# Attention scores with 128 contraction rows, in two products instead of three, and the second head pair's projections in other PSUM banks

## The reference, cut to what matters

```python
z = jnp.einsum('bqhd,bkhd->bhqk', q_blk.astype(jnp.float32), kf) * scale
# stick-breaking heads
strict = key_pos[None, :] < q_pos[:, None]
log_beta = jax.nn.log_sigmoid(z)
...
# forgetting heads (q and k are RMS-normalised per head first)
z = z + jnp.moveaxis(f_q, 1, 2)[..., None] - f_keys[:, :, None, :]
p = jax.nn.softmax(jnp.where(causal, z, -jnp.inf), axis=-1)
```

## Time and profile before

| | |
|---|---|
| median of 3 runs | 1152.43 us (1151.81 to 1153.05) |
| profiled execution, its own time | 1151.13 us |
| its span | 1149.4 us |
| mean granted clock of TensorE | 0.998 |
| PE busy | 1129.6 us (98%) |
| DVE busy | 582.7 us (51%) |
| ACT busy | 435.9 us (38%) |
| POOL busy | 62.3 us (5%) |
| the mixer, about | 422 to 727 us of the span |

### The profile page before, as it was taken

The page is one execution under the profiler, slowest core; times in us unless marked ns, Lnnn a source line. Parts: engine busy times, 40 slices in busy tenths (PEclk is TensorE's granted clock), DMA queues, the critical chain, the costliest instruction groups (busy, mean ns, idle before and its releaser), DMA issues.

```text
span 1149.4 us, 14368 instructions
## 1 busy us (share of the span) xinstructions
PE 1129.6 (98%) x5206; PEld 896.3 (78%) x5206; DVE 582.7 (51%) x813; ACT 435.9 (38%) x677; POOL 62.3 (5%) x48
## 2 busy tenths in 40 slices
PE   8999999999999998999999999999999999999997
PEld 5788888888788867788778777778888888878876
DVE  3745555555644465666665566673333333433343
ACT  5422222222222234566775665352232322221322
POOL 1000000000000001000000000000000000225350
PEclk9999999999999999999999999999999999999999
DMA  9655765675573731222212111332333333223231
GB/s 344 209 147 164 204 198 164 166 202 164 165 212 106 192 91 40 71 56 56 55 38 68 44 37 37 92 92 74 91 91 91 91 91 94 89 65 110 83 110 74
DMA packets 168918, 131.21 MB, mean 114 GB/s; under 512 B 5180, under 2 KB 150700, under 8 KB 168876
## 3 DMA queue, kind: packets, MB, share of 16 engines
q1 hardware_dynamic: 168704, 130.60, 38.8%
q10 hardware_dynamic: 172, 0.06, 0.0%
HBM read 128.54 MB, written 2.10 MB: 114 GB/s over the span
## 4 chain that ended last, share of the span: by engine, by line
PE 93%; DVE 3%; ACT 2%; DMA 1%; issue 1%; DVEq 0%; POOL 0%; SPq 0%; ACTq 0%; POOLq 0%
PE bank L662 29%; PE bank L664 28%; PE bank L663 28%; PE bank L950 1%; PE bank L975 1%; PE bank L682 1%; DVE w_lo L1424 1%; DMA w_raw<-in_w_ffn_down_dram 1%; PE bank L928 1%; ACT w_hi L1070 1%; PE bank L715 1%; PE bank L1008 0%; PE bank L708 0%; DVE y L1879 0%; PE bank L740 0%
## 5 line engine op out<-in xcount | busy, mean ns | idle before, releaser
L1424 DVE TENSOR_TENSOR w_lo<-w_raw,w_hi 128x1024 fp32r<-128x1024 f32 x163 | 215.1, 1321 | 387.9 <-ACT w_hi L1070 387.7
L662 PE MATMUL bank<-h_hi,w_hi 128*128 128x512 f32 x864 | 350.0, 405 | 3.9 <-DVE v_lo L1725 3.6
L664 PE MATMUL bank<-h_hi,w_lo 128*128 128x512 f32 x864 | 342.9, 397 | 0.0
L663 PE MATMUL bank<-h_lo,w_hi 128*128 128x512 f32 x864 | 342.9, 397 | 0.0
L1070 ACT ACTIVATE w_hi<-w_raw 128x1024 fp32r<-128x1024 f32 x163 | 172.2, 1058 | 424.7 <-PE bank L664 396.0
L662 PEld LDWEIGHTS bank<-h_hi,w_hi 128*128 128x128 f32 x864 | 163.3, 189 | 46.9 <-issue 8.1
L663 PEld LDWEIGHTS bank<-h_lo,w_hi 128*128 128x128 f32 x864 | 163.3, 189 | 40.7 <-issue 2.9
L664 PEld LDWEIGHTS bank<-h_hi,w_lo 128*128 128x128 f32 x864 | 163.1, 189 | 39.5
L563 POOL TENSOR_TENSOR w_raw<-w_raw,gate_row 128x1024 f32<-128x1024 f32 (+1 forms) x24 | 56.0, 2334 | 627.2 <-DMA w_raw<-in_w_ffn_down_dram 626.8
L662 PE MATMUL bank<-w_hi,hid_hi 128*128 128x512 f32 x176 | 69.8, 397 | 2.2 <-DVE w_lo L1424 2.2
L662 PE MATMUL bank<-hid_hi,w_hi 128*128 128x512 f32 x176 | 70.2, 399 | 1.3 <-DVE w_lo L1424 1.3
(11 more groups left out here) (201 smaller groups left out, 1339.9 us busy)
## 6 DMA issues: line engine op xcount, KB each, us to landing
w_raw<-in_w_ffn_up_dram SPq DMA_DIRECT2D x88, 512.0 KB, 4.8
ada_w<-in_w_ada_dram SPq DMA_DIRECT2D x56, 512.0 KB, 3.8
w_raw<-in_w_ffn_down_dram SPq DMA_DIRECT2D x36, 512.0 KB, 4.5
w_raw<-in_w_in_dram SPq DMA_DIRECT2D x28, 512.0 KB, 3.9
ada_first<-in_w_ada_dram SPq DMA_DIRECT2D x16, 512.0 KB, 10.2
w_raw<-in_w_out_dram SPq DMA_DIRECT2D x8, 512.0 KB, 3.7
w_raw<-in_w_ffn_down_dram SPq DMA_DIRECT2D x8, 384.0 KB, 4.7
x_nat<-in_x_dram SPq DMA_DIRECT2D x4, 512.0 KB, 4.8
```

Of the source, the lines that this page charges most:

```text
L662: mm(dst, wh, xh, start=start, stop=False, skip_group_check=skip)
L663: mm(dst, wh, xl, start=False, stop=False, skip_group_check=skip)
L664: return mm(dst, wl, xh, start=False, stop=stop, skip_group_check=skip)
L1424: v.tensor_tensor(w_lo[:, s, :], w_raw[:, r, :], w_hi[:, s, :].bitcast(F32), ALU.subtract)\
```

## The change

The stationary operand of a segment gets 128 rows: the head's high part of q in its own 64 partitions and the low part in the other 64 (`q_st`). The moving operand of the first product is the high part of k in both halves (`k_hh`): its second half is made by a transfer inside SBUF that GpSimd issues (`repeat_k`), once ACT has written the high part (`k_made`). The moving operand of the second product is the low part of k with zero rows in the other half (`k_l`). These two replace the three. ACT and DVE write the parts in two instructions of 64 partitions each instead of one of 128. GpSimd clears the zero rows when FFN 1's last tile has been used, and issues the first job's copies between its memsets. `f_cum` and `rowsel` get 128 rows, of which the new ones are zero. q1 and k1 are put in banks 6 and 7, and the values and statistics of job 0 wait until those have been read. `k_hh` and `k_l` of even jobs lie in the room of the last heads' outputs, and the split of v0's first weight tile lies in that of the first.

```diff
-        out.append((kind, n, {"v": 0, "q": 0, "k": 1, "g": n % 2}[kind] + (6 if kind in "qk" and n == 0 else 0), tile))
+        out.append((kind, n, {"v": 0, "q": 0, "k": 1, "g": n % 2}[kind] + (6 if kind in "qk" and n <= 1 else 0), tile))
...
-        rowsel_f = keep("rowsel_f", [HD, JOBS])
-        rowsel = keep("rowsel", [HD, JOBS], F32R)
+        rowsel_f = keep("rowsel_f", [P, JOBS])
+        rowsel = keep("rowsel", [P, JOBS], F32R)
...
-        qk_hi = keep("qk_hi", [P, 2, 2, SEQ], F32R)
-        qk_lo = keep("qk_lo", [P, 2, 2, SEQ], F32R)
+        q_st = keep("q_st", [P, 2, 2, SEQ], F32R)
+        k_hh_b = keep("k_hh_b", [P, 2, SEQ], F32R)
+        k_l_b = keep("k_l_b", [P, 2, SEQ], F32R)
         pt_hi = keep("pt_hi", [P, 2, PT_BLOCKS, P], F32R)
         pt_lo = keep("pt_lo", [P, 2, PT_BLOCKS, P], F32R)
+        o_offset = top[0]
         o_hi = keep("o_hi", [P, JOBS, SEQ], F32R)
         o_lo = keep("o_lo", [P, JOBS, SEQ], F32R)
+        k_hh_a = at("k_hh_a", [P, 2, SEQ], F32R, o_offset + (JOBS - 2) * SEQ * 4)
+        k_l_a = at("k_l_a", [P, 2, SEQ], F32R, o_offset + (2 * JOBS - 2) * SEQ * 4)
+        k_hh, k_l = (k_hh_a, k_hh_b), (k_l_a, k_l_b)
         beyond = top[0]
         f_keys = keep("f_keys", [P, 2, SEQ])
-        f_cum = keep("f_cum", [HD, SEQ], F32R)
+        f_cum = keep("f_cum", [P, SEQ], F32R)
...
-        w4_hi = at("w4_hi", [P, WS], F32R, region + 2 * FC * SEQ * 4)
-        w4_lo = at("w4_lo", [P, WS], F32R, region + 2 * FC * SEQ * 4 + WS * 4)
+        w4_hi = at("w4_hi", [P, WS], F32R, o_offset)
+        w4_lo = at("w4_lo", [P, WS], F32R, o_offset + WS * 4)
...
-        mix_zero = sem("mix_zero")
+        mix_zero, k_zero = sem("mix_zero"), sem("k_zero")
+        k_twice = [sem("k_twice0"), sem("k_twice1")]
...
+        def k_made(j):
+
+            if j >= SBJ:
+                return nrm_hi, norm_of("k", j) + 1
+            ci = [c for c, chunk in enumerate(CHUNKS) if chunk[0:2] == ("k", j)][0]
+            until = STEPS.index(("evac", ci))
+            return chunk_hi, 1 + sum({"v": 2, "q": 1, "k": 1, "g": 0}[CHUNKS[step[1]][0]]
+                                     for step in STEPS[:until] if step[0] == "evac")
+
...
+            def repeat_k(j):
+
+                pool.wait_ge(*k_made(j))
+                g.dma_start(k_hh[j % 2][HD:P, 0, :].bitcast(F32), k_hh[j % 2][0:HD, 0, :].bitcast(F32))\
+                    .then_inc(k_twice[j % 2], 16)
+                g.dma_start(k_hh[j % 2][0:HD, 1, :].bitcast(F32), k_hh[j % 2][HD:P, 1, :].bitcast(F32))\
+                    .then_inc(k_twice[j % 2], 16)
+
+            pool.wait_ge(w_used, T_MIX)
+            for n, part in enumerate((k_l_a[HD:P, 0, :], k_l_a[0:HD, 1, :], k_l_b[HD:P, 0, :], k_l_b[0:HD, 1, :])):
+                g.memset(part.bitcast(F32), 0.0).then_inc(k_zero, 1)
+                pool.wait_ge(k_zero, n + 1)
+
             pool.wait_ge(h_done, 2 * KC)
...
                 pool.wait_ge(mix_zero, n + 1)
+                if n == 0:
+                    repeat_k(0)
+            for j in range(1, JOBS):
+                repeat_k(j)
...
+                        if j == 0:
+                            pe.wait_ge(k_zero, 4)
+                        pe.wait_ge(k_twice[j % 2], 32 * (j // 2 + 1))
...
-                        rows = slice(h * HD, (h + 1) * HD)
-                        q_h, q_l = (q[rows, j % 2, 0, i * P:(i + 1) * P] for q in (qk_hi, qk_lo))
-                        k_h, k_l = (k[rows, j % 2, 1, 0:n] for k in (qk_hi, qk_lo))
-                        three(zb[:, c0:c0 + n], q_h, q_l, k_h, k_l, True, False)
+                        qs = q_st[:, j % 2, h, i * P:(i + 1) * P]
+                        mm(zb[:, c0:c0 + n], qs, k_hh[j % 2][:, h, 0:n], start=True, stop=False)
+                        mm(zb[:, c0:c0 + n], qs, k_l[j % 2][:, h, 0:n], start=False, stop=False)
...
+                        pe.wait_ge(*chunk_read(last_on_bank[6]))
...
+                    else:
+                        pe.wait_ge(*chunk_read(last_on_bank[7]))
...
-                    mm(bank[7][:], rowsel[:, head:head + 1].broadcast_to([HD, P]), f_cum[:], start=True, stop=True)\
+                    mm(bank[7][:], rowsel[:, head:head + 1].broadcast_to([P, P]), f_cum[:], start=True, stop=True)\
...
-                        a(qk_hi[:, n % 2, int(what == "k"), :], bank[b][:], ACT.Copy,
-                          scale=0.125 if what == "q" else 1.0).then_inc(chunk_hi, 1)
+                        for h in range(2):
+                            rows = slice(h * HD, (h + 1) * HD)
+                            if what == "q":
+                                last = a(q_st[rows, n % 2, h, :], bank[b][rows, :], ACT.Copy, scale=0.125)
+                            else:
+                                last = a(k_hh[n % 2][rows, h, :], bank[b][rows, :], ACT.Copy)
+                        last.then_inc(chunk_hi, 1)
...
-                        a(qk_hi[:, n % 2, int(what == "k"), :], nrm[:], ACT.Copy,
-                          scale=gq8[:] if what == "q" else col(R_GK)).then_inc(nrm_hi, 1)
+                        for h in range(2):
+                            rows = slice(h * HD, (h + 1) * HD)
+                            if what == "q":
+                                last = a(q_st[rows, n % 2, h, :], nrm[rows, :], ACT.Copy, scale=gq8[rows, :])
+                            else:
+                                last = a(k_hh[n % 2][rows, h, :], nrm[rows, :], ACT.Copy, scale=col(R_GK)[rows, :])
+                        last.then_inc(nrm_hi, 1)
...
-                        v.scalar_tensor_tensor(qk_lo[:, n % 2, int(what == "k"), :], bank[b][:],
-                                               0.125 if what == "q" else 1.0,
-                                               qk_hi[:, n % 2, int(what == "k"), :].bitcast(F32),
-                                               ALU.mult, ALU.subtract).then_inc(qk_ready, 1)
+                        for h in range(2):
+                            rows, other = slice(h * HD, (h + 1) * HD), slice((1 - h) * HD, (2 - h) * HD)
+                            if what == "q":
+                                last = v.scalar_tensor_tensor(q_st[other, n % 2, h, :], bank[b][rows, :], 0.125,
+                                                              q_st[rows, n % 2, h, :].bitcast(F32),
+                                                              ALU.mult, ALU.subtract)
+                            else:
+                                last = v.tensor_tensor(k_l[n % 2][rows, h, :], bank[b][rows, :],
+                                                       k_hh[n % 2][rows, h, :].bitcast(F32), ALU.subtract)
+                        last.then_inc(qk_ready, 1)
...
-                        v.scalar_tensor_tensor(qk_lo[:, n % 2, int(what == "k"), :], nrm[:],
-                                               gq8[:] if what == "q" else col(R_GK),
-                                               qk_hi[:, n % 2, int(what == "k"), :].bitcast(F32),
-                                               ALU.mult, ALU.subtract).then_inc(nrm_lo, 1)
+                        for h in range(2):
+                            rows, other = slice(h * HD, (h + 1) * HD), slice((1 - h) * HD, (2 - h) * HD)
+                            if what == "q":
+                                last = v.scalar_tensor_tensor(q_st[other, n % 2, h, :], nrm[rows, :], gq8[rows, :],
+                                                              q_st[rows, n % 2, h, :].bitcast(F32),
+                                                              ALU.mult, ALU.subtract)
+                            else:
+                                last = v.scalar_tensor_tensor(k_l[n % 2][rows, h, :], nrm[rows, :], col(R_GK)[rows, :],
+                                                              k_hh[n % 2][rows, h, :].bitcast(F32),
+                                                              ALU.mult, ALU.subtract)
+                        last.then_inc(nrm_lo, 1)
```

## The result

The changed kernel takes 1145.63 us (median of 5 runs, 1145.08 to 1148.20). The kernel before took 1152.43 us on the same chip (5 runs, 1151.56 to 1154.29). The ratio is 0.9943, 95% interval 0.9928 to 0.9958: faster by 6.8 us, where 26.2 were forecast, and outside the range of 1121 to 1138. The profiled execution took 1145.88 us, its span is 1144.1.

A forecast was written before the change was run, and what follows sets the result against it. The prediction took the mixer for a PE-bound stream. Gross savings of 10.2 + 7.8 + 6.0 + 1.6 + 5.3 = 30.9 us less 4.7 of losses gave 26.2, so 1126.2 us, range 1121 to 1138.

The forecast's parts named there:

- The products removed: Scores on PE: one product fewer in each of 64 segments, 10.2 us saved.
- the ways in: Scores on PE: entering 64-row products after transposes or a mask costs extra; 7.8 us saved, bounds 0 and 7.8.
- the ways out: Scores on PE, second product to mask: leaving 64-row products costs extra; 6.0 us saved, bounds 0 and 6.0.
- rival A: Scores on PE: float transposes and bfloat mask, not height, cause the extra time; gain 11, 1141 us; chance 0.12.
- the late weight load: Mask product on PE: its weight load starting late looked like a drain, so the full 6.0 us was taken.
- The banks' term: Job 0, q1 and k1 in banks 6 and 7: the v0 wait and low clock behind it go, 5.3 us.
- rival C: First scores of five jobs: copies come late; gain 7 at 8.1 us, 1159 us at 11 us; chance 0.05.
- decay products: Eight PE products going from 64 to 128 rows, an entry and an exit each: 1.6 us saved, bounds 0 and 1.6.
- theory L: Formed after the measurement: in jobs 0 to 3 a closed DVE and ACT loop, longer than PE's shortened unit, lost the gain.
- just met: Statistics products after a head's values: six of sixteen have little slack before a PE that comes earlier, 1.5 us lost.
- Rival B: Mixer: evacuations' second halves aren't hidden, PE waits 10 us more at transposes and statistics; gain 16, 1136 us; chance 0.13.
- Job 0's start: Job 0's first transposes and weight tiles: split evacuations make ACT and DVE later, 2.2 us lost, bounds 0 and 5.

The follow-up runs named there:

- banks-only kernel: The kernel before with only q1 and k1 in banks 6 and 7 and the two waits that guard them: 1147.61 us, ratio 0.9955.
- both remedies: Changed kernel with q and k evacuations in one 128-partition instruction per engine and the absolute value ahead of relu; scores partly of wrong rows: 1123.55 us, ratio 0.9759.
- one-piece kernel: Changed kernel with q's and k's parts written in one instruction of 128 partitions on ACT and on DVE; scores of other numbers: 1130.20 us.
- absolute value first: Changed kernel with ACT's absolute value as soon as a unit's scores are made and DVE's relu after it: 1132.87 us, ratio 0.9827.
- one piece on DVE: Changed kernel with DVE's low parts of q and k in one 128-partition instruction, ACT's high parts still in two: 1134.37 us, ratio 0.9848.
- one piece on ACT: Changed kernel with ACT's high parts of q and k in one 128-partition instruction, DVE's low parts in two: 1141.12 us, ratio 0.9909.
- experiment 4: The kernel before with q and k evacuations in two 64-partition instructions on ACT and on DVE, nothing else changed: 1158.36 us, ratio 1.0053.

## Why the prediction was wrong

**What held.** The products removed, the ways in and the ways out have their spacings in the rows above, so rival A is out. The prediction's argument from the late weight load was wrong, though: the load is as late with 128 rows, and only the spacing shrank. The Trainium skill (TensorEngine Tiling (Array Packing), Tiling Modes, Key Properties) says that a change of tiling mode drains TensorE; the trace agrees, with 0.12 to 0.17 us on the way in and 0.09 to 0.10 on the way out. The banks' term was 5.3 and measured 4.9. The copies were hidden, in job 0 with nothing to spare, so rival C is out: 2.5 to 2.6 us each, where the estimate from the Trainium skill (DMA: Bandwidth & Descriptors, Anatomy of one DMA) was 2.3.

The gross sum holds term by term. Start to start over the whole mixer, from the banks-only kernel to the one with both remedies, the 64 removed products and the ways out take 17.4 us less (forecast 10.2 + 6.0), the ways in 7.9 (7.8) and the eight decay products 1.8 (1.6). With the banks' 4.9 that is 32.0, and the gross was 30.9. The kernel with both remedies agrees as a whole: its span is 1121.0 us, 28.4 under that of before, and its PE waits beside the removed one are 2.2 us more than before (3.2 against 4.6 - 3.6 = 1.0), 30.6 together.

**The step that failed** is the one on what is added on ACT and DVE: "Most of it lies beside PE's projections and costs nothing; without that cover it would be 0.6 to 0.7 us per evacuation." It was argued from shares of 69% and 74%. All losses together were priced at 4.7 us and measured 30.9 - 6.8 = 24.1. Shares say how much an engine works, not how long its round is. Two things were missed. The pieces aren't hidden: 15.4 us. And DVE's round is too long for the shortened stream even without them: the one-piece kernel is 5 to 7 us behind the one with both remedies (1130.20 against 1123.55, and 5.3 by the ratios), and the prediction had no term for that. The banks-only kernel shows the round before the pieces, one unit of DVE from relu to relu:

```profile
467.90 0.68 DVE L1782 TENSOR_SCALAR tmp_b<-bank 128x512 f32<-128x512 f32 x1
470.64 1.28 DVE L1810 TENSOR_TENSOR_SCAN tmp_b<-tmp_a,tmp_b 128x384 f32<-128x384 f32 x2 [2.06 <-ACT tmp_a L1334]
...
472.56 0.68 DVE L1741 SCALAR_TENSOR_TENSOR qk_lo<-bank,qk_hi 128x512 fp32r<-128x512 f32 x1
473.16 1.21 DVE L1427 TENSOR_TENSOR w_lo<-w_raw,w_hi 128x1024 fp32r<-128x1024 f32 x1
...
474.95 0.68 DVE L1782 TENSOR_SCALAR tmp_b<-bank 128x512 f32<-128x512 f32 x1
```

That is 7.05 us with the idle 2.06 in it. With two pieces, a low part takes 1.42 us to the next start and not 0.60, and the round is 8.00. PE's unit is shorter once the scores are cheap: over the first twenty units, transposes to transposes, the kernel with both remedies takes 6.70 us a unit on average, the one with the absolute value first 6.80, and the kernel before, its waits included, 7.70. From the first to the last relu of jobs 0 to 3 the kernel before takes 139.4 us, the banks-only kernel 134.9, the changed kernel 137.0 and the one with the absolute value first 124.7. So the change took work from PE in those jobs, and DVE's loop ran 2.1 us slower than with the banks' edit alone.

**What became of the 24.1 us.** 21 to 22 come back with the two remedies, neither of which touches PE's work. Where they lie shows when PE's timeline is cut at job 4's first transposes (us from job 0's first scores to there, and from there to the mixer's end):

| kernel | jobs 0 to 3 | jobs 4 to 7 |
|---|---|---|
| before | 162.3 | 121.7 |
| banks only | 157.7 | 122.6 |
| changed | 161.3 | 117.4 |
| changed, absolute value first | 146.6 | 117.9 |
| changed, one piece | 151.7 | 111.3 |
| changed, one piece on DVE | 152.9 | 114.7 |
| changed, one piece on ACT | 159.3 | 114.5 |
| changed, both remedies | 144.5 | 111.6 |

Against the kernel with both remedies the changed kernel loses 16.8 us in jobs 0 to 3, where the loop is. The absolute value brings 14.7 of them back, DVE's one piece 8.4 and ACT's 2.0, as theory L has it. In jobs 4 to 7 there is no relu and no such loop, and 5.8 us are lost all the same: there the absolute value changes nothing, and the piece on either engine costs 2.7 to 2.9. The waits behind job 4's first transposes are 2.0 us for the squares on ACT, 1.4 for `pt_lo` and 1.0 for `f_keys`, where 0.3 stay with both remedies. So some three quarters of the loss lie where theory L applies. The rest are waits of the kind that the prediction called just met and priced at 1.5 us; what makes them longer there wasn't taken apart further.

By kind: of the 23.1 us by which the spans of the changed kernel and of the one with both remedies differ, 22.5 lie between matching products of the mixer. Of these, 3.0 are in the two stretches at 1.2 GHz, and 18.9 are at the products that had to wait. The view of waits lists 15.7 for the same products. It counts only PE's idle time, and a product that comes late also loses its overlap with the one before: the one at 476.29 is listed with 2.92 us, but starts 3.3 us behind its predecessor, where 0.23 is plain.

**Rival B** had the mechanism, ACT and DVE become the bound, and was given 0.13. Its price was 16 x 0.6 = 10 us and 1136 us. It counted a piece once where it is executed, and nothing for the loop's own idle 2.06 us. Pieces in a stream with slack of a fraction of a microsecond cost 5.9 us (experiment 4), in the shortened stream 15.4, and 8 to 9 where the loop is short (1132.87 - 1123.55, and 7.8 by the ratios); of these the table has 6.3 in jobs 4 to 7. The order of PE's steps came out as I read it. Job 0's start, priced at 2.2, was about right as long as no loop is behind: transposes wait 0.76 and 0.65 us there for `tmp_b`, and a projection 0.22 for a weight tile; the first long wait is the value products' at 476.29. The statistics, priced at 1.5, measured 5.0 (`ssum`), and 1.0 more for `f_keys`.

**What had stood in the profile of before.** The earlier trace rows show an ACT instruction that begins behind a DVE instruction, and the earlier trace rows that PE waited little. What was missing was to walk one unit of DVE from relu to relu, and to set its length without waits beside PE's new unit. The trace of before has such units in job 1:

```profile
488.15 0.68 DVE L1779 TENSOR_SCALAR tmp_b<-bank 128x512 f32<-128x512 f32 x1
490.89 1.27 DVE L1807 TENSOR_TENSOR_SCAN tmp_b<-tmp_a,tmp_b 128x384 f32<-128x384 f32 x2 [2.06 <-ACT tmp_a L1331]
...
495.55 0.68 DVE L1779 TENSOR_SCALAR tmp_b<-bank 128x512 f32<-128x512 f32 x1
```

That is 7.40 us. PE's unit was 7.70 with the 5.3 us of the one wait and its clock in it, and 7.4 without. The change was to take 25.6 / 40 = 0.6 us from it, which leaves 6.8: less than DVE's round, even before a second piece is added to that.

## What to carry to other kernels

Before costing work on a side engine at nothing, walk one period of that engine in its own order: sum the starts, its idle time behind a third engine included, and leave out only what waits for the bound engine. If that length plus the addition is more than the bound engine's period after the change, the loss can be as much as the difference in every period, and busy shares of 70% don't show it. Here 20 x (8.00 - 6.70) = 26 us is such a bound, and 16.8 were lost, since not every round is that long. And where two engines alternate, look for a wait that carries no data: here one instruction's order within a unit was worth 12.8 us once the bound engine was fast, and about 1 us, not told from nothing, before.

## What was not expected of the hardware

An ACT or DVE instruction on 64 partitions costs what one on 128 does, 0.59 and 0.69 us at 512 columns, which was forecast; but two DVE halves in sequence take 1.42 us to the next start where the one takes 0.60, so 0.82 and not 0.69 more. GpSimd is busy 0.52 to 0.69 us issuing one transfer of 128 KB inside SBUF. The waits of PE of 2.9 and 2.0 us were each followed by 3.4 us at 1.2 GHz, but the length of the wait alone doesn't decide: in the kernel with one piece on DVE a wait of 2.0 us, at 486.3, stands in a mixer whose mean granted clock is 1.00. And the weight load of the bfloat mask product begins only 0.01 us ahead of it, with 128 rows of float before it as with 64.
